# A head's root-mean-square norm, spread over one more slot of the attention loop of block 1

## The chip, the cores and the metric

The kernel runs on one core of a Trainium2 chip. The metric is the device time of one execution in microseconds. Lower is better.

## The reference, cut to what matters

The program computes two transformer blocks one after the other, all in fp32. The change touches only the first, which has two layers (0 and 1). In each layer attention has eight heads of a first kind (A) and four of a second kind (B), and only the second kind has a norm of its own:

```
def diff_attend(q1, q2, k1, k2, v, lam):        # heads of the second kind, 4 of them
    p = softmax(q1 k1 / 8) - lam * softmax(q2 k2 / 8)
    return p @ v                                 # 128 numbers per token and head

def mixer_outputs(o_a, o_b, ga, gb, p, lam_init):
    y_a = o_a.reshape(B, S, H_A * V_A) @ p['w_br_a']
    o_b = rms_norm(o_b, p['g_sub']) * (1.0 - lam_init)    # the norm of this change, over the 128
    y_b = o_b.reshape(B, S, H_B * V_B) @ p['w_br_b']
    merged = sigmoid(ga) * y_a + sigmoid(gb) * y_b
    return merged @ p['w_out']
```

Layer 0 has 512 latent and 256 context tokens as queries, layer 1 the 512 latent tokens only.

## The kernel before, in words

Every engine runs a fixed list of instructions, in order, and engines meet at semaphores. For the heads of a layer all five lists come from one list of items, `head_items` (L310 to L419), which `pe_heads`, `act_heads` and `dve_heads` walk. The list goes slot by slot. A slot is one chunk of 256 keys of one pair of query tiles (256 queries); a pair over 768 keys has three slots. In a slot stand: `scores` of tiles two or three slots ahead (q times k into PSUM; VectorE takes the row maxima at L1448, ScalarE the exponentials at L1291, and for the second kind VectorE weighs the two softmaxes together, the item `weigh`, ending at L1363); `turn` (TensorE transposes the weights, L1170; ScalarE copies the result out, L1301, and VectorE takes its low half, L1462); `values` of the slot two before (L1184 broadcasts the inverse sums, L1203 to L1205 multiply by v; after a pair's last chunk ScalarE copies the sum out, L1315, and VectorE scales it, L1479); and pieces of later work: projections of the next head (`b_qk`, 24 matmuls at L658 to L660), its rotation (`b_rope`: L1139 and L1140 on TensorE, L1431 to L1436 on VectorE, L1276 on ScalarE), early `gate` projections (24 matmuls, copied out by ScalarE at L1324), and `prepare`, the split of a weight block (L618 on ScalarE, L629 on VectorE).

The norm of a head of the second kind is four items. `ob_square`: ScalarE squares a pair's scaled sum (L1330). `ob_sum`: TensorE sums the squares over the partitions with a matrix of ones, one matmul per stream (L1217; the stream of 512 and in layer 0 also that of 256). `ob_root`: ScalarE takes the logarithm out of PSUM (L1336) and then the exponential of minus half of it (L1340), with a load of the function table ahead of each. `ob_norm`: VectorE multiplies the head by it (L1486), and the SyncE queue stores it. Heads are numbered 0 to 11; 8 to 11 are of the second kind.

Where results of `turn`, `gate`, `b_qk`, `b_rope` and `ob_sum` go is fixed by a ring, `gen = Turns([4, 5, 7])`: three PSUM banks, taken in turn in TensorE's order. Who takes a bank waits until the one before has given it back:

```
def take(self, queue, *key, place=None):
    ...
    if self.held[i] is not None and self.given_back is not None:
        name, event = self.given_back[self.held[i]]
        queue.wait_ge(self.signals[name], *event)
```

An `ob_sum` gives its bank back with the logarithm (`logged`), a `b_rope` with VectorE's addition at L1433 (`roped`), a `turn` and a `b_qk` with VectorE's reading of it (`taken`), a `gate` with ScalarE's copy (`copied`).

Of the kernel before, what the change touches and what calls it, by code (L numbers as in the profile page):

```python
# [246 lines left out]
def early_gates(streams):  # L247
    return [(m, s, g) for m in EARLY for s, g in itertools.product(streams, range(2))]
# [37 lines left out]
def pairs_of(streams):  # L286

    out = []
    for n, (kind, h) in enumerate(HEADS):
        for s in streams:  # L290
            for q0 in range(s[0], s[1], 2 * P):
                keys = N_TOK if s == LAT else N_CTX
                out.append(dict(n=n, kind=kind, h=h, s=s, q0=q0, keys=keys, chunks=keys // (2 * P), i=len(out)))
    return out
# [15 lines left out]
def head_items(layer, engine):  # L310


    streams = [LAT] if layer == DEPTH - 1 else [LAT, CTX]
    pairs = pairs_of(streams)
    slots = [(p["i"], c) for p in pairs for c in range(p["chunks"])]
    first = {i: x for x, (i, c) in enumerate(slots) if c == 0}
    per_head = len(pairs) // len(HEADS)

    def pieces(n):

        kind, h = HEADS[n]
        if kind == "A":
            steps = [[("a_q", n, h, s)] for s in streams] + [[("a_k", n, h, s)] for s in (LAT, CTX)]
            if h == 3:
                steps[len(streams) - 1].append(("prepare",))
            if h == H_A - 1:
                steps[-1].append(("prepare",))
            return steps
        steps = []
        if h == 0:  # L330
            for b in range(2):
                steps += [[("v_b", b, t)] for t in range(N_TOK // P)]
                if b == 0:
                    steps[1].append(("prepare",))
                steps[-1].append(("prepare",))
        steps += [[("b_qk", n, h, 0, s)] for s in streams] + [[("b_rope", n, h, 0)]]
        steps += [[("b_qk", n, h, 1, s)] for s in (LAT, CTX)] + [[("b_rope", n, h, 1)]]
        steps[-2].append(("prepare",))
        return steps

    plan = [dict(scores=[], pieces=[]) for _ in slots]
    start, at = [], 0
    for p in pairs:
        for a in range(2):
            t = 2 * p["i"] + a
            if p["i"] == 0:
                start.append(("scores", t))
                continue
            at = max(at, first[p["i"]] - 3 + a)
            plan[at]["scores"].append(("scores", t))  # L350
    scored = {t: x for x, slot in enumerate(plan) for _, t in slot["scores"]}
    for n in range(1, len(HEADS)):
        steps = pieces(n)
        lo = scored.get(2 * per_head * (n - 1) - 1, -1) + 1 if n > 1 else 0
        hi = scored[2 * per_head * n] - 1
        for i, step in enumerate(steps):
            plan[lo + i * (hi - lo) // len(steps)]["pieces"].append(step)

    gates = [[] for _ in slots]
    second_kind = first[H_A * per_head]  # L360
    for x, of_chunk in zip(GATE_AT[len(streams)], EARLY):
        for y, key in zip(x, [(m, s, g) for m, s, g in early_gates(streams) if m == of_chunk]):
            gates[second_kind + y].append(("gate",) + key)
        gates[second_kind + x[-1]].append(("prepare",))

    out = []
    for i, step in enumerate(pieces(0)):
        if i == len(streams):
            out += [("v_a", t) for t in range(N_TOK // P)]
        out += step  # L370
        out += [("late",) + x for x in step if x[0] in ("a_q", "a_k")]
    out += start
    second = {2 * p["i"] + a for p in pairs for a in range(2) if p["kind"] == "B"}
    late, weigh, values, ob = [], [], [], {}

    def of_values(x, i, c):

        p = pairs[i]
        out.append(("values", i, c))
        if c == p["chunks"] - 1 and p["kind"] == "B":  # L380
            ob.setdefault("ob_square", []).append((x, i))
            if (i + 1) % per_head == 0:
                for what in ("ob_sum", "ob_root", "ob_norm"):
                    ob.setdefault(what, []).append((x + 1, p["n"]))

    def of_norm(x, what):
        out.extend((what, y) for at, y in ob.get(what, ()) if at == x)

    for x, (i, c) in enumerate(slots):
        scores = plan[x]["scores"]  # L390
        if engine != "act":
            out += scores[0:1]
        out.append(("turn", i, c))
        out += late
        late = []
        of_norm(x, "ob_sum")
        values.append((i, c))
        if len(values) > 2:
            of_values(x, *values.pop(0))
        if engine == "act":  # L400
            out += scores[0:1]
        out += [("weigh", t) for t in weigh]
        weigh = [t for _, t in scores if t in second]
        of_norm(x, "ob_root")
        out += gates[x]
        late += [("gate_out",) + y[1:] for y in gates[x] if y[0] == "gate"]
        for step in plan[x]["pieces"]:
            out += step
            late += [("late",) + y for y in step if y[0] in ("a_q", "a_k")]
        out += scores[1:]  # L410
        of_norm(x, "ob_norm")
        of_norm(x, "ob_square")
    out += late
    for x, y in enumerate(values, len(slots)):
        of_values(x, *y)
        of_norm(x, "ob_square")
    for what in ("ob_sum", "ob_root", "ob_norm"):
        of_norm(len(slots) + len(values), what)
    return out  # L419


def build(nc, dram, out, book):

    with ExitStack() as ctx:
# [657 lines left out]
        def pe_heads(l):  # L1082
# [7 lines left out]
            for s in mine(l):  # L1090
                for k in range(3):
                    pe.wait_ge(taken, "cq", l, k, s)
            for item in head_items(l, "pe"):
                what, at = item[0], item[1:]
                if what == "a_q":
# [134 lines left out]
        def act_heads(l):  # L1230
            pairs = pairs_of(mine(l))
            chunks, chunk_no = chunk_numbers(pairs)
            act.wait_ge(wide_out)
            for item in head_items(l, "act"):
                what, at = item[0], item[1:]
                if what == "prepare":
# [105 lines left out]
        def dve_heads(l):  # L1342
# [22 lines left out]

            dve.wait_ge(normed, "ckv", l, 1, CTX)
            for item in head_items(l, "dve"):
                what, at = item[0], item[1:]
                if what == "prepare":
# [2064 lines left out]
```

## Time and profile before

| | us |
|---|---|
| median of 3 runs | 3739.1 (3736.39 to 3739.17) |
| span of the profiled execution | 3735.9 |
| TensorE busy | 3440.3 (92%) |
| VectorE busy | 1890.1 (51%) |
| ScalarE busy | 1431.1 (38%) |
| GpSimd busy | 309.1 (8%) |

The profiled execution has a span of 3735.9 us from its first to its last instruction, and the runs' median is 3.2 us above that. TensorE is busy nearly all the time; the others have long stretches in which they wait for it. All times in the trace are from the span's start. The second-kind heads of layer 0 lie at about 430 to 590 us, those of layer 1 at about 1720 to 1845 us.

### The profile page before, as it was taken

The page shows a single profiled execution, that of the slowest core. Times are in us where ns is not written, and L with a number is a line of the kernel's source. Part 1 is how long each engine was busy: PE and PEld are TensorE (multiplying, and loading weights), DVE is VectorE, ACT ScalarE, POOL GpSimd, SP SyncE. Part 2 cuts the span into 40 slices and gives each one's busy share as a digit, 9 for nine tenths or more (in the row PEclk, how much of TensorE's full clock was granted, in tenths as well). Part 3 has the DMA queues.
Part 4 walks back from the last instruction along what each step waited for, and adds up shares of the span by engine and source line. Part 5 has one row for each costly group of instructions (what it writes and reads, how often), then busy time and mean ns, then how long its engine had stood idle before and what let it go on. Part 6 is the DMA issues. An engine that isn't in the chain of part 4 may idle for free.

```text
span 3735.9 us, 42555 instructions
## 1 busy us (share of the span) xinstructions
PE 3440.3 (92%) x17738; PEld 2877.4 (77%) x17738; DVE 1890.1 (51%) x2678; ACT 1431.1 (38%) x2194; POOL 309.1 (8%) x242
## 2 busy tenths in 40 slices
PE   7898898999999988899799999879999888979997
PEld 6778777888888876787687888757887776758885
DVE  5674654777636545655545544544333555343233
ACT  4563444233313335534534333433222345352222
POOL 0000000221001110000011001220000200220002
PEclk9999999999999999999999999989999889999999
DMA  5101114433324321011242322212222111112222
GB/s 205 34 22 60 51 45 147 156 124 129 108 80 141 120 74 40 30 59 49 88 147 102 116 104 85 97 68 84 94 102 96 62 43 34 46 46 98 102 91 69
DMA packets 74495, 321.96 MB, mean 86 GB/s; under 512 B 8896, under 2 KB 17856, under 8 KB 52288
## 3 DMA queue, kind: packets, MB, share of 16 engines
q1 hardware_dynamic: 74304, 319.25, 24.8%
q8 instruction: 140, 2.29, 0.3%
q14 instruction: 51, 0.42, 0.0%
HBM read 303.49 MB, written 15.73 MB: 85 GB/s over the span
## 4 chain that ended last, share of the span: by engine, by line
PE 50%; DVE 4%; ACT 4%; POOL 1%; issue 1%; DMA 0%; POOLq 0%; ACTq 0%; DVEq 0%; SPq 0%
PE psum L658 14%; PE psum L660 14%; PE psum L659 14%; POOL arena L1988 1%; PE psum L1158 1%; DVE split_weights L629 1%; PE psum L671 1%; ACT split_weights L618 1%; PE psum L672 1%; PE psum L673 1%; PE psum L1170 1%; DVE arena L1448 0%; PE psum L2720 0%; PE psum L2696 0%; PE psum L1184 0%
## 5 line engine op out<-in xcount | busy, mean ns | idle before, releaser
L658 PE MATMUL psum<-split_inputs,split_weights 128*128 128x512 f32 (+1 forms) x2872 | 1054.6, 367 | 12.5 <-DVE split_weights L629 8.5
L659 PE MATMUL psum<-split_inputs,split_weights 128*128 128x512 f32 (+1 forms) x2872 | 1046.1, 364 | 0.0
L660 PE MATMUL psum<-split_inputs,split_weights 128*128 128x512 f32 (+1 forms) x2872 | 1045.0, 364 | 0.0
L629 DVE TENSOR_TENSOR split_weights<-arena,split_weights 128x2048 fp32r<-128x2048 f32 (+3 forms) x246 | 508.4, 2066 | 428.5 <-ACT split_weights L618 428.0
L658 PEld LDWEIGHTS psum<-split_inputs,split_weights 128*128 128x128 f32 x2872 | 545.2, 190 | 105.2 <-DVE split_weights L629 11.6
L659 PEld LDWEIGHTS psum<-split_inputs,split_weights 128*128 128x128 f32 x2872 | 544.9, 190 | 87.2 <-issue 3.0
L660 PEld LDWEIGHTS psum<-split_inputs,split_weights 128*128 128x128 f32 x2872 | 544.1, 189 | 86.0
L618 ACT ACTIVATE split_weights<-arena 128x2048 fp32r<-128x2048 f32 (+3 forms) x246 | 413.9, 1683 | 159.0 <-PE psum L660 158.9
L658 PE MATMUL psum<-split_hidden,split_weights 128*128 128x512 f32 (+1 forms) x880 | 324.1, 368 | 1.0 <-DVE split_weights L629 0.9
L659 PE MATMUL psum<-split_hidden,split_weights 128*128 128x512 f32 (+1 forms) x880 | 323.9, 368 | 0.0
L660 PE MATMUL psum<-split_hidden,split_weights 128*128 128x512 f32 (+1 forms) x880 | 323.7, 368 | 0.0
L2018 ACT ACTIVATE arena<-psum 128x512 f32<-128x512 f32 (+2 forms) x120 | 66.5, 557 | 367.1 <-PE psum L660 346.9
L658 PEld LDWEIGHTS psum<-split_hidden,split_weights 128*128 128x128 f32 x880 | 165.9, 189 | 29.5 <-DVE split_weights L629 2.1
L660 PEld LDWEIGHTS psum<-split_hidden,split_weights 128*128 128x128 f32 x880 | 165.9, 188 | 27.6
L659 PEld LDWEIGHTS psum<-split_hidden,split_weights 128*128 128x128 f32 x880 | 165.9, 189 | 27.5
L680 ACT ACTIVATE arena<-arena 128x512 f32<-128x512 f32 (+1 forms) x134 | 78.0, 590 | 275.9 <-DVE arena L1840 97.9
L1158 PE MATMUL psum<-split_high 128*128 128x512 f32 (+3 forms) x864 | 143.5, 366 | 43.6 <-ACT arena L1291 41.5
L1516 DVE CUSTOM_DVE_ANT_0 arena<-arena 128x1024 f32<-128x1024 f32 x128 | 165.2, 1290 | 28.2 <-DMA arena<-w_ada_dram 24.3
L1448 DVE TENSOR_REDUCE arena<-psum 128x1 f32<-128x768 f32 (+1 forms) x160 | 132.0, 846 | 77.1 <-PE psum L1158 76.2
L1158 PEld LDWEIGHTS psum<-split_high 128*128 128x128 f32 (+1 forms) x864 | 114.5, 205 | 72.9 <-ACT arena L1291 38.8
L703 POOL TENSOR_TENSOR arena<-arena 128x512 f32<-128x512 f32 x66 | 84.1, 1280 | 1002.7 <-ACT arena L680 1002.7
L1291 ACT ACTIVATE arena<-psum,arena 128x768 f32<-128x768 f32 (+1 forms) x160 | 130.2, 816 | 65.6 <-DVE arena L1448 62.4
(340 smaller groups left out, 4953.2 us busy)
## 6 DMA issues: line engine op xcount, KB each, us to landing
arena<-w_up_dram SPq DMA_DIRECT2D x44, 1024.0 KB, 5.7
arena<-ffn_up_dram SPq DMA_DIRECT2D x44, 1024.0 KB, 4.8
arena<-w_ada_dram SPq DMA_DIRECT2D x80, 512.0 KB, 3.7
arena<-w_in_dram SPq DMA_DIRECT2D x32, 1024.0 KB, 4.8
arena<-w_down_dram SPq DMA_DIRECT2D x32, 704.0 KB, 4.1
arena<-ffn_down_dram SPq DMA_DIRECT2D x32, 704.0 KB, 4.1
arena<-od_w_in_dram SPq DMA_DIRECT2D x13, 1024.0 KB, 4.9
arena<-w_ada_dram SPq DMA_DIRECT2D x8, 1024.0 KB, 12.7
```

What stands on the lines that cost most here:

```text
L618: act.e.activation(ws[:, i % N_SLOTS, 0, 0:nk * w], raw_view(key), ACT.Copy).then_inc(*w_hi(*key))
L629: dve.e.tensor_tensor(ws[:, i, 1, 0:nk * w], raw_view(key), ws[:, i, 0, 0:nk * w].bitcast(F32), ALU.subtract).then_inc(*w_lo(*key))
L658: pe.e.matmul(dst, a[0], b[0], start=i == 0, stop=False)
L659: pe.e.matmul(dst, a[0], b[1], start=False, stop=False)
L660: ins = pe.e.matmul(dst, a[1], b[0], start=False, stop=i == n - 1)
L680: act.e.activation(row, view, ACT.Square, **more).then_inc(*squared(site, s, c))
L703: pool.e.tensor_tensor(acc, acc, rows.at(site, s, c)[:, 0:w], ALU.add).then_inc(*rows.back((site, s, c), pooled, site, s, c))
L1158: ins.append(pe.e.matmul(dst, a[rows_at, :], b[rows_at, :], start=i == 0, stop=i == 2))
L1291: act.e.activation(row[:, 0:p["keys"]], psum[:, b:b + p["keys"]], ACT.Exp, bias=st[:, sub:sub + 1], accum_out=st[:, 2 + sub:3 + sub]).then ...
L1448: dve.e.tensor_reduce(st[:, sub:sub + 1], psum[:, b:b + p["keys"]], AX.X, ALU.max, negate=True).then_inc(*maxed(l, t, sub))
L1516: dve.e.tensor_tensor_reduce(part.get("junk", rstd_all), ADA[slots[n % len(slots)]], wide[:, s, :], 1.0, 0.0, ALU.mult, ALU.add, mods[al][ ...
L2018: act.e.activation(dst, banks.at(*key)[:, cols], func, **more).then_inc(*banks.back(key, copied, *key))
```

## The change

A norm whose last pair ends with `values` in slot x (where its `ob_square` also stands) was summed, rooted and scaled in slot x + 1: `ob_sum` right behind that slot's `turn`, `ob_root` in the middle, `ob_norm` near the end. Now `ob_sum` stands near the end of slot x + 1, behind its pieces of later work, and `ob_root` and `ob_norm` in slot x + 2. The last head of a layer keeps its order, so three heads in each layer (8, 9 and 10) change: six places. No instruction is added or removed.

```
         if c == p["chunks"] - 1 and p["kind"] == "B":
             ob.setdefault("ob_square", []).append((x, i))
             if (i + 1) % per_head == 0:
-                for what in ("ob_sum", "ob_root", "ob_norm"):
-                    ob.setdefault(what, []).append((x + 1, p["n"]))
+                ob.setdefault("ob_sum", []).append((x + 1, p["n"]))
+                for what in ("ob_root", "ob_norm"):
+                    ob.setdefault(what, []).append((x + 2, p["n"]))
 
     def of_norm(x, what):
         out.extend((what, y) for at, y in ob.get(what, ()) if at == x)
@@ -393,7 +394,6 @@
         out.append(("turn", i, c))
         out += late
         late = []
-        of_norm(x, "ob_sum")
         values.append((i, c))
         if len(values) > 2:
             of_values(x, *values.pop(0))
@@ -409,13 +409,16 @@
             late += [("late",) + y for y in step if y[0] in ("a_q", "a_k")]
         out += scores[1:]
         of_norm(x, "ob_norm")
+        of_norm(x, "ob_sum")
         of_norm(x, "ob_square")
     out += late
-    for x, y in enumerate(values, len(slots)):
-        of_values(x, *y)
+    for x in range(len(slots), len(slots) + len(values) + 2):
+        of_norm(x, "ob_root")
+        of_norm(x, "ob_norm")
+        if x < len(slots) + len(values):
+            of_values(x, *values[x - len(slots)])
+        of_norm(x, "ob_sum")
         of_norm(x, "ob_square")
-    for what in ("ob_sum", "ob_root", "ob_norm"):
-        of_norm(len(slots) + len(values), what)
     return out
```

Behind the diff every line number of the changed kernel is 3 higher: L1217 is L1220, L1170 is L1173, L1184 is L1187, L1139 is L1142, L1158 is L1161, L658 is L661; on ScalarE L1336 is L1339, L1340 is L1343, L1276 is L1279, L1301 is L1304, L1291 is L1294, L1324 is L1327, L1315 is L1318.

First TensorE in layer 0 around head 8's sum (L1217), from slot x + 1's transposes (L1170) to the first gate matmul of slot x + 2 (L658); the groups left out are the matmuls of `values`. Before:

```order
L1170 MATMUL psum<-arena 128x128 x3
L1217 MATMUL psum<-arena 128x512 [waits squared,taken]
L1217 MATMUL psum<-arena 128x256 [waits squared,taken]
L1184 MATMUL psum<-arena 128x128 [waits stat,scaled]
...
L1139 MATMUL psum<-split_high 128x512 [waits taken]
L1140 MATMUL psum<-split_high 128x512
L1158 MATMUL psum<-split_high 128x256 [waits exped]
L1158 MATMUL psum<-split_high 128x256 x5
L1170 MATMUL psum<-arena 128x128 [waits weighed,logged]
...
L658 MATMUL psum<-split_inputs,split_weights 128x512 [waits logged,w_lo]
```

and in the changed kernel:

```order
L1173 MATMUL psum<-arena 128x128 x3
L1187 MATMUL psum<-arena 128x128 [waits stat,scaled]
...
L1142 MATMUL psum<-split_high 128x512 [waits taken]
L1143 MATMUL psum<-split_high 128x512
L1220 MATMUL psum<-arena 128x512 [waits squared,taken]
L1220 MATMUL psum<-arena 128x256 [waits squared,taken]
L1161 MATMUL psum<-split_high 128x256 [waits exped]
L1161 MATMUL psum<-split_high 128x256 x5
L1173 MATMUL psum<-arena 128x128 [waits weighed,roped]
...
L661 MATMUL psum<-split_inputs,split_weights 128x512 [waits logged,w_lo]
```

The two sums went behind `b_rope` (L1142, L1143). The transposes of slot x + 2 now wait for `roped` where they waited for `logged`. The gate's matmul waits for `logged` in both, but the ring of three banks gives it the bank of the first sum where it had that of the second.

Then ScalarE at the same place, from the copy of slot x + 1's transposes (L1301) to the copy of the gate (L1324). Before:

```order
L1301 ACTIVATE split_low<-psum 128x512 [waits turned]
L1336 ACT_TABLE_LOAD
L1336 ACTIVATE arena<-psum,arena 128x512 [waits product]
L1336 ACTIVATE arena<-psum,arena 128x256 [waits product]
L1340 ACT_TABLE_LOAD
L1340 ACTIVATE arena<-arena 128x768 [waits logged]
L1276 ACTIVATE split_high<-arena 128x512 [waits roped]
L1301 ACTIVATE split_high<-psum 128x512 [waits turned,product]
L1291 ACTIVATE arena<-psum,arena 128x256 [waits maxed]
L1291 ACTIVATE arena<-psum,arena 128x256 [waits maxed,weighed]
L1324 ACTIVATE arena<-psum 128x512 [waits product,gate_stored_0_loaded]
```

and in the changed kernel:

```order
L1304 ACTIVATE split_low<-psum 128x512 [waits turned]
L1279 ACTIVATE split_high<-arena 128x512 [waits roped]
L1304 ACTIVATE split_high<-psum 128x512 [waits turned,product]
L1294 ACTIVATE arena<-psum,arena 128x256 [waits maxed]
L1294 ACTIVATE arena<-psum,arena 128x256 [waits maxed,weighed]
L1339 ACT_TABLE_LOAD
L1339 ACTIVATE arena<-psum,arena 128x512 [waits product]
L1339 ACTIVATE arena<-psum,arena 128x256 [waits product]
L1343 ACT_TABLE_LOAD
L1343 ACTIVATE arena<-arena 128x768 [waits logged]
L1327 ACTIVATE arena<-psum 128x512 [waits product,gate_stored_0_loaded]
```

The two logarithms and the exponential, with both table loads, went behind the copy of the next transposes and the exponentials of the next scores (L1294).

Last ScalarE at head 10 of layer 1, near the end of that layer's heads, where no gate is left. Before:

```order
L1301 ACTIVATE split_low<-psum 128x512 [waits turned]
L1336 ACT_TABLE_LOAD
L1336 ACTIVATE arena<-psum,arena 128x512 [waits product]
L1340 ACT_TABLE_LOAD
L1340 ACTIVATE arena<-arena 128x512 [waits logged]
L1301 ACTIVATE split_high<-psum 128x512 [waits turned,product] x2
L1315 ACTIVATE arena<-psum 128x256 [waits ob_stored_1_loaded,product]
```

and in the changed kernel:

```order
L1304 ACTIVATE split_low<-psum 128x512 [waits turned]
L1304 ACTIVATE split_high<-psum 128x512 [waits turned,product]
L1339 ACT_TABLE_LOAD
L1339 ACTIVATE arena<-psum,arena 128x512 [waits product]
L1343 ACT_TABLE_LOAD
L1343 ACTIVATE arena<-arena 128x512 [waits logged]
L1304 ACTIVATE split_high<-psum 128x512 [waits turned,product]
L1318 ACTIVATE arena<-psum 128x256 [waits ob_stored_1_loaded,product]
```

The group of four for the root went past one copy of transposes and stands right ahead of the next copy and of L1318, the copy of a finished pair out of PSUM.

## Rows read from the trace of the kernel before

**Rows 1.** The page: its span.

```profile
span 3735.9 us, 42555 instructions
```

**Rows 2.** Waits of TensorE, 430 to 600 us: total, times, longest.

```profile
PE psum L1158 <- ACT arena L1291: 6.2, 2, 3.1
PE psum L1217 <- ACT arena L1330: 4.7, 4, 1.4
```

**Rows 3.** Waits of TensorE, 1720 to 1846 us.

```profile
PE psum L1217 <- ACT arena L1330: 6.7, 4, 2.5
```

**Rows 4.** Timeline, TensorE, head 8 of layer 0: start, length, instructions, idle before.

```profile
456.66 0.49 PE L1139 MATMUL psum<-split_high 128*128 128x512 f32 x1 [0.70 <-DVE split_low L1462]
...
458.14 0.63 PE L1170 MATMUL psum<-arena 128*128 128x128 f32 x4 [0.19 <-DVE arena L1363]
...
459.32 0.39 PE L658 MATMUL psum<-split_inputs,split_weights 128*128 128x512 f32 x1
```

**Rows 5.** Timeline, VectorE, the same place.

```profile
456.97 1.02 DVE L1363 SCALAR_TENSOR_TENSOR arena<-arena 128x768 f32<-128x768 f32 x1
...
458.63 0.69 DVE L1433 TENSOR_TENSOR arena<-arena,psum 128x512 f32<-128x512 f32 x1
...
460.63 1.01 DVE L1486 SCALAR_TENSOR_TENSOR arena<-arena 128x768 f32<-128x768 f32 x1
461.56 0.75 DVE L1448 TENSOR_REDUCE arena<-psum 128x1 f32<-128x256 f32 x2
```

**Rows 6.** Timeline, ScalarE, the same place.

```profile
454.50 1.28 ACT L1336 ACT_TABLE_LOAD   x1
455.79 1.05 ACT L1336 ACTIVATE arena<-psum,arena 128x512 f32<-128x512 f32 x2
...
462.83 0.20 ACT L1291 ACTIVATION_READ_ACCUMULATOR arena<-psum,arena 128x1 f32 x1
```

**Rows 7.** Instructions of line L1336: shortest, median, longest in ns.

```profile
L1336 ACT ACTIVATE arena<-psum,arena x12: 468/688/692, 455.8 to 1839.8; 128x512 f32<-128x512 f32 x8, 128x256 f32<-128x256 f32 x4
```

**Rows 8.** Timeline, TensorE, head 10 of layer 0.

```profile
562.02 0.67 PE L1217 MATMUL psum<-arena 128*128 128x256 f32 x2 [1.34 <-ACT arena L1330]
...
569.26 0.62 PE L1158 MATMUL psum<-split_high 64*128 64x256 f32 x6
...
571.01 0.28 PE L658 MATMUL psum<-split_inputs,split_weights 128*128 128x256 f32 x1
```

**Rows 9.** Timeline, ScalarE, the same place.

```profile
571.80 0.21 ACT L1291 ACTIVATION_READ_ACCUMULATOR arena<-psum,arena 128x1 f32 x1
```

**Rows 10.** Timeline, TensorE, head 10 of layer 1.

```profile
1821.77 0.50 PE L1158 MATMUL psum<-split_high 64*128 64x512 f32 x2 [3.33 <-ACT arena L1291]
...
1827.04 2.05 PE L1217 MATMUL psum<-arena 128*128 128x512 f32 x2 [2.20 <-ACT arena L1330]
...
1830.76 0.60 PE L1170 MATMUL psum<-arena 128*128 128x128 f32 x4
...
1834.31 0.71 PE L1184 MATMUL psum<-arena 128*128 128x128 f32 x4 [0.62 <-DVE arena L1479]
```

**Rows 11.** Timeline, VectorE, the same place.

```profile
1828.47 1.02 DVE L1363 SCALAR_TENSOR_TENSOR arena<-arena 128x768 f32<-128x768 f32 x1
1831.79 0.75 DVE L1486 SCALAR_TENSOR_TENSOR arena<-arena 128x512 f32<-128x512 f32 x1 [2.30 <-ACT arena L1340]
...
1833.85 0.41 DVE L1479 TENSOR_TENSOR arena<-arena,psum 128x256 f32<-128x256 f32 x1
```

**Rows 12.** Timeline, ScalarE, the same place.

```profile
1831.13 0.63 ACT L1340 ACTIVATE arena<-arena 128x512 f32<-128x512 f32 x1
1831.66 0.58 ACT L1301 ACTIVATE split_high<-psum 128x512 fp32r<-128x512 f32 x1
```

**Rows 13.** Windows at half clock: us, busy of each engine, granted clock.

```profile
475.30:482.10 6.80, 5.48 (x27) 5.08 (x28) 3.21 (x8) 2.96 (x8) 0.00 (x0) 0.50 0.00 0
536.80:540.20 3.40, 3.25 (x17) 2.85 (x18) 0.95 (x2) 0.32 (x2) 0.00 (x0) 0.50 0.03 7
```

More of the change, by code:

```diff
@@ L382, in of_values @@
             if (i + 1) % per_head == 0:
-                for what in ("ob_sum", "ob_root", "ob_norm"):
-                    ob.setdefault(what, []).append((x + 1, p["n"]))
+                ob.setdefault("ob_sum", []).append((x + 1, p["n"]))
+                for what in ("ob_root", "ob_norm"):
+                    ob.setdefault(what, []).append((x + 2, p["n"]))
     def of_norm(x, what):
@@ L395, in head_items @@
         late = []
-        of_norm(x, "ob_sum")
         values.append((i, c))
@@ L411, in head_items @@
         of_norm(x, "ob_norm")
+        of_norm(x, "ob_sum")
         of_norm(x, "ob_square")
     out += late
-    for x, y in enumerate(values, len(slots)):
-        of_values(x, *y)
+    for x in range(len(slots), len(slots) + len(values) + 2):
+        of_norm(x, "ob_root")
+        of_norm(x, "ob_norm")
+        if x < len(slots) + len(values):
+            of_values(x, *values[x - len(slots)])
+        of_norm(x, "ob_sum")
         of_norm(x, "ob_square")
-    for what in ("ob_sum", "ob_root", "ob_norm"):
-        of_norm(len(slots) + len(values), what)
     return out
```

## The prediction

> **What bounds the kernel now.** I read the views in this order: the page, the waits of TensorE in the two stretches where the changed heads lie, then the timelines of TensorE, VectorE and ScalarE at each of the six places. The page gives the span, 3735.9 us [rows 1]; TensorE is busy for 3440.3 us of it, so what delays TensorE delays the end, unless a later wait of TensorE on something that is not behind it takes the delay up. In the heads of layer 0 the reader sees what the change is aimed at: TensorE waits 4.7 us in four pieces at the norm's sums for ScalarE's squares [rows 2], and in layer 1 another 6.7 us in four [rows 3]. Of the eight pieces six belong to heads 8 to 10 and two to head 11, which keeps its order. So less than 4.7 + 6.7 = 11.4 us stand at the moved instructions. The timelines then show what TensorE would wait for next if those waits were gone: at head 8 of layer 0 it stops 0.70 us for VectorE's low half of the transposes and 0.19 us for its weighing [rows 4].
>
> **The change part by part.** No instruction is added or removed. What moves is the sum (12 matmuls in the program, of which 9 move), and with it who holds which of the three banks; then the two table loads, the logarithms, the exponential, the scaling and the store. I go through the places.
>
> *Head 8 of layer 0 (and head 9, whose rows repeat these some 60 us later).* TensorE skips the first wait of 1.37 us and does the head's `values` and `b_rope` at once. The second sum then needs the bank of slot x + 1's transposes, which VectorE gives back where L1139 could start before, at 456.66 [rows 4]. So nothing is won there: scores 58 start about where they did. Now the transposes of slot x + 2. Before, they got the bank of the first sum, long given back. Now they get that of `b_rope`, which VectorE gives back when L1433 ends, 458.63 + 0.69 = 459.32 [rows 5]. A semaphore from VectorE takes some 0.15 us (L1363 ends at 456.97 + 1.02 = 457.99, and TensorE goes on at 458.14 [rows 4, 5]), so they start at 459.5 instead of 458.14, 1.3 us late. VectorE doesn't get later, since all it does up to there depends on itself and on ScalarE.
>
> Then the gate. From the transposes to the gate TensorE needs 459.32 - 458.14 = 1.18 us [rows 4], so it is at the gate at 460.7. The gate needs the bank of the first sum, which the logarithm gives back, and the logarithm now stands behind the exponentials of scores 58. Those come earlier than before, because L1486 no longer stands ahead of the maxima on VectorE: 461.56 - 460.63 = 0.93 us [rows 5]. ScalarE's last row there ended at 462.83 + 0.20 = 463.03 [rows 6], so now at 462.1. Then a table load of 1.28 us [rows 6], the first logarithm of 0.69 us [rows 7] and a semaphore: 462.1 + 1.28 + 0.69 + 0.15 = 464.2. The gate starts at 464.2 instead of 459.32: **4.9 us late**, of which 3.5 us are idle in one piece. For heads 8 and 9 of layer 0 that makes 9.8 us. The cover that hid the root before was TensorE's own work from the sums to the gate and an idle ScalarE; now the root starts 7.6 us after 454.50 and has none. The gate's 24 matmuls hide the second load, the exponential, L1486 and the store on the SyncE queue. What stands behind the store there, the store of the gate's result, waits for the gate anyway.
>
> *Head 10 of layer 0.* No `b_rope` here, and a gate follows `values` at once. Its bank is free, so TensorE doesn't wait 1.34 us at the sum [rows 8] and reaches scores 70 at 569.26 - 1.34 = 567.9. ScalarE's last exponential row ended 571.80 + 0.21 - 569.26 = 2.75 us after those scores began [rows 8, 9], so at 570.65 now; with load, logarithm and semaphores (1.28 + 0.69 + 0.15) the gate's bank is free at 572.8, where the gate started at 571.01 [rows 8]: **1.75 us late**, 3.1 us idle in one piece.
>
> *Head 8 of layer 1.* One stream and one sum. The sum goes behind `b_qk`, 24 matmuls, and its wait, the smallest (2.5 and 2.20 of the 6.7 us stand elsewhere [rows 3, 10], and head 11 has a part), is gone. But ten microseconds later VectorE is behind: the next low halves and maxima follow on a weight split, and L1486, 0.75 us long [rows 11], now stands in that row of work instead of ahead of it. I count a gain of 0.1 us.
>
> *Head 9 of layer 1.* The wait of 2.5 us at the sum [rows 3] shrinks to 1.3 us, since ScalarE splits a weight block ahead of the squares and `values` fills no more than 1.2 us; behind the scores, the transposes wait for VectorE's weighing, which is not moved. It ends when it did. 0 us.
>
> *Head 10 of layer 1.* No gate follows. The 2.20 us at the sum and the slow 2.05 us of the sum [rows 10] go; the next transposes are set free by the weighing, 1828.47 + 1.02 + 0.15 = 1829.64 [rows 11], not at 1830.76 [rows 10], 1.1 us early. But the root now stands right ahead of what the pair's end needs. ScalarE begins their copy some 0.7 us later and has them by 1830.95, then comes load, logarithm, load, exponential, 1.28 + 0.69 + 1.28 + 0.63 = 3.9 us [rows 6, 7, 12], to 1834.85. Behind it wait the next copy of transposes (0.58 us [rows 12]) and the copy L1315, and on VectorE behind L1486 (0.75 us) a low half (0.7 us, as the 0.69 us of L1433 at the same width [rows 5]) and L1479 (0.41 us [rows 11]), for which TensorE waits at L1184. 1834.85 + 0.75 + 0.7 + 0.41 gives 1836.7 with its semaphores, where L1184 started at 1834.31 [rows 10]: **2.4 us late**, all of it on the way to the end of the layer's heads.
>
> Sum without the clock: 9.8 + 1.75 - 0.1 + 0 + 2.4 = 13.8 us.
>
> *The clock.* The two stops of 3.1 us at L1158 in layer 0's heads [rows 2] are both followed by a stretch at half clock (1.2 instead of 2.4 GHz), with 5.48 and 3.25 us of TensorE's work in it [rows 13], of which half, 2.7 and 1.6 us, is lost. The stop of 3.33 us in layer 1 was followed at once by matmuls at full speed [rows 10], so a stop this long costs between 0 and 2.7 us; the mean of the three is 1.4 us. The change makes four such stops: 3.5, 3.5, 3.1 and, at head 10 of layer 1, 3.3 us. The first three have a long gate behind them and I count 1.4 us each, 4.3 us; the last has little work behind it, and I count nothing. The Trainium skill ("TensorE: Matmul & The Clock Gate", Terms) puts the penalty at the throttled time times one minus K/N, so at half of it; by that and the trace it is the same price.
>
> Total: 13.8 + 4.3 = 18.1 us over the profiled execution, whose own runs lie 3.2 us above its span (3739.1 - 3735.9). 3739.1 + 18.1 = **3757 us**.
>
> A place where page and trace differ: the load stands in the new wait three times and twice in the last place. The rows show 1.28 us, and the logarithm follows 454.50 + 1.28 + 0.01 later [rows 6]. The Trainium skill ("ScalarE: Activation LUTs", What ACT_TABLE_LOAD costs) adds a drain of about 1.38 us to each switch, 2.66 us in all. By the page the delay would be 5 x 1.38 = 6.9 us more, 3764 us; the trace has no such gap, and I go by the trace.
>
> **The rivals.** *The banks don't decide, and the waits are gone (faster).* If the logarithm of the first sum ended before TensorE reached the gate, the gain would be what VectorE's weighing leaves of the waits at the sums: 1.3 us at head 10 of layer 0 and 1.1 us at head 10 of layer 1, up to the whole 11.4 us: 3728 to 3736.7 us. For it speaks that the waits at the sum are real and that ScalarE is the least busy of the three. It decides at 460.7: the logarithm must have ended by then, and it would have to end 3.5 us earlier than its order allows, since an engine doesn't pass an instruction that waits. 4 in 100.
>
> *The delay is taken up later (within 0.2%).* The next stops of TensorE, 3.1 us at L1158 [rows 2], would have to shrink by what the gate is late. They would if ScalarE or VectorE were behind there; but both wait for TensorE's gate right before, so the whole row of work moves. Or two of the steps fail: head 8 and 9 of layer 0 at 2 us each make 3739.1 + 4 + 4 - 1.3 = 3745 us. 6 in 100.
>
> *Main case, slower*: 90 in 100. Its own bounds are 3739.1 + 13.8 = 3752.9 with no loss of clock and 3739.1 + 13.8 + 4 x 2.7 = 3763.7 with the dearest at each stop.
>
> **How the numbers follow.** The runs tell a change from none at about 0.2%, 7.5 us. The predicted time is the main case's. The range goes from 3749 us (one of the two big stalls 4 us smaller than worked out, without loss of clock) to 3764 us. Of 10 in 100 outside the main case nearly all lie below it, and some 8 in 100 of the main case outside its bounds. Faster 4, same 6, slower 90 in 100.
>
> **What the changed profile would show.** In the waits of TensorE, L661 (the gate) for ScalarE's logarithm L1339, three times, 3.5, 3.5 and 3.1 us; L1173 for VectorE's rotation (L1436 in the new numbers) two times, 1.3 us; nearly nothing at L1220 in layer 0 for the squares; L1187 in layer 1 for L1482, over 3 us once. Half-clock stretches behind some gates. What would make it wrong: a gate that starts right behind `values`, or later stops at L1161 that are shorter than before by what the gates lost.

## The result, and the profile after

The changed kernel takes 3759.04 us (median of 4 runs, 3755.66 to 3759.23); the kernel before took 3738.86 us beside it. The ratio is 1.0052, 95% interval 1.0037 to 1.0066: slower by 20.2 us. The profiled execution has a span of 3757.3 us, 21.4 more than before [rows 1].

TensorE's waits in the second-kind heads of layer 0, which lie at 430 to 610 us now; total, times, longest:

```profile
PE psum L661 <- ACT arena L1339: 9.6, 4, 2.9
PE psum L1161 <- ACT arena L1294: 6.2, 2, 3.1
PE psum L1173 <- DVE arena L1436: 2.9, 2, 1.5
PE psum L1220 <- DVE split_low L1465: 2.3, 1, 2.3
PE psum L1220 <- DVE split_high L1465: 2.3, 1, 2.3
PE psum L1220 <- ACT arena L1333: 0.6, 1, 0.6
```

The wait of the sums for the squares fell from 4.7 us [rows 2] to 0.6 us, head 11's. In its place stand the sum's wait for VectorE's low half of the transposes (4.6 us, which took in the 1.4 us of heads 8 and 9 at L1139, 0.70 us each [rows 4]), the transposes' wait for the rotation (2.9 us) and the gate's wait for the logarithm (9.6 us, of which 1.8 us is the merge's first gate, as before).

Head 8 of layer 0, TensorE's timeline (start, length, idle before and its releaser):

```profile
455.06 0.70 PE L1220 MATMUL psum<-arena 128*128 128x256 f32 x2 [2.28 <-DVE split_low L1465]
...
457.77 1.12 PE L1173 MATMUL psum<-arena 128*128 128x128 f32 x4 [1.46 <-DVE arena L1436]
...
462.63 0.77 PE L661 MATMUL psum<-split_inputs,split_weights 128*128 128x512 f32 x1 [2.47 <-ACT arena L1339]
```

and ScalarE's:

```profile
460.29 0.20 ACT L1294 ACTIVATION_READ_ACCUMULATOR arena<-psum,arena 128x1 f32 x1
460.51 1.28 ACT L1339 ACT_TABLE_LOAD   x1
461.80 1.05 ACT L1339 ACTIVATE arena<-psum,arena 128x512 f32<-128x512 f32 x2
```

This execution came to these heads 1.6 us earlier than the one before. With that, L1173 is 457.77 - 458.14 + 1.6 = 1.2 us late and the gate 462.63 - 459.32 + 1.6 = 4.9 us [rows 4]. The three rows of ScalarE are the chain to read: last exponential row, load, logarithm, with nothing between them, and the gate right behind the first of the two logarithms. Head 9 repeats it.

Head 10 of layer 1, TensorE's timeline:

```profile
1843.57 0.63 PE L1173 MATMUL psum<-arena 128*128 128x128 f32 x4 [1.56 <-DVE arena L1366]
...
1850.61 1.23 PE L1187 MATMUL psum<-arena 128*128 128x128 f32 x4 [3.00 <-DVE arena L1482]
```

From the transposes freed by the weighing to the values of the last pair there are 1850.61 - 1843.57 = 7.04 us now, where there were 1834.31 - 1830.76 = 3.55 us [rows 10].

And the clock, in windows (length, busy time of TensorE, its weight loads, VectorE, ScalarE and GpSimd, then the granted clock):

```profile
456.70:466.90 10.20, 6.66 (x20) 5.53 (x21) 3.95 (x7) 6.60 (x11) 0.00 (x0) 0.50 0.18 76
482.00:485.40 3.40, 3.38 (x29) 3.13 (x30) 2.06 (x3) 1.62 (x4) 0.00 (x0) 1.00 0.02 5
1849.30:1856.10 6.80, 5.07 (x22) 4.77 (x22) 1.95 (x4) 1.59 (x5) 0.00 (x0) 0.50 0.10 39
```

The first is a stretch at half clock (1.2 of 2.4 GHz) that the kernel before doesn't have at this place: it begins between the new stops and reaches into the gate. The second lies right behind the next stop of 3.09 us at L1161. There the clock is full now; the kernel before had half clock behind the same stop [rows 13]. The third begins in the stop of 3.00 us at L1187 and outlasts it by 5.5 us.

Where the 21.4 us of the two profiled executions lie, by the same five marks in each (the first 3.09 us stop at L1158, the first gate of layer 0's merge, the 2.11 us stop at which layer 1's second-kind heads begin, the first gate of layer 1's merge, the end):

| stretch | before, us | changed, us | more |
|---|---|---|---|
| up to 417.23 / 415.59 | 417.2 | 415.6 | -1.6 |
| heads of layer 0, up to 590.24 / 602.60 | 173.0 | 187.0 | +14.0 |
| up to 1656.29 / 1668.41 | 1066.1 | 1065.8 | -0.2 |
| heads of layer 1, up to 1840.62 / 1859.10 | 184.3 | 190.7 | +6.4 |
| the rest | 1895.3 | 1898.2 | +2.9 |

The first, the third and the last stretch hold no changed instruction, and half clock differs in them: 37.5 us in the first stretch before and 34.1 us now, 161.3 and 174.1 us in the last. So up to 3 us either way comes without any change of the lists in that stretch. A second trace of the changed kernel, on another chip, gives 187.0 and 190.8 us for the two stretches of heads, so these two are the change's. It also gives 1898.2 us for the last stretch again: whether part of its 2.9 us comes with the change is not shown.

### The profile page after: what moved, and what is told of

Its sections match the earlier page's. It is cut to its first block, busy times and chain, and to the rows that moved or that the text cites. A ratio compares the mean times of both kernels' runs of the same rounds, so it can differ in the third digit from the quotient of the medians.

```text
span 3757.3 us, 42554 instructions
## 1 busy us (share of the span) xinstructions
PE 3452.1 (92%) x17738; PEld 2887.2 (77%) x17738; DVE 1889.8 (50%) x2678; ACT 1429.6 (38%) x2194; POOL 308.5 (8%) x242
## 4 chain that ended last, share of the span: by engine, by line
PE 50%; DVE 4%; ACT 4%; POOL 1%; issue 1%; DMA 0%; POOLq 0%; ACTq 0%; DVEq 0%; SPq 0%
PE psum L661 14%; PE psum L662 14%; PE psum L663 14%; POOL arena L1991 1%; PE psum L1161 1%; DVE split_weights L632 1%; PE psum L674 1%; PE psum L675 1%; PE psum L676 1%; PE psum L1173 1%; ACT split_weights L621 1%; PE psum L2699 0%; DVE arena L1451 0%; PE psum L2723 0%; PE psum L1187 0%
## 5 line engine op out<-in xcount | busy, mean ns | idle before, releaser
L661 PE MATMUL psum<-split_inputs,split_weights 128*128 128x512 f32 (+1 forms) x2872 | 1057.3, 368 | 20.3 <-ACT arena L1339 9.6
L661 PEld LDWEIGHTS psum<-split_inputs,split_weights 128*128 128x128 f32 x2872 | 547.1, 190 | 113.8 <-issue 12.0
L661 PE MATMUL psum<-split_hidden,split_weights 128*128 128x512 f32 (+1 forms) x880 | 324.2, 368 | 0.1
L661 PEld LDWEIGHTS psum<-split_hidden,split_weights 128*128 128x128 f32 x880 | 165.9, 189 | 28.6 <-DVE split_weights L632 0.9
L1161 PE MATMUL psum<-split_high 128*128 128x512 f32 (+3 forms) x864 | 142.5, 363 | 43.6 <-ACT arena L1294 41.4
L1161 PEld LDWEIGHTS psum<-split_high 128*128 128x128 f32 (+1 forms) x864 | 113.6, 203 | 73.9 <-ACT arena L1294 38.8
L1294 ACT ACTIVATE arena<-psum,arena 128x768 f32<-128x768 f32 (+1 forms) x160 | 130.0, 815 | 62.4 <-DVE arena L1451 58.3
```

The source lines that it names most:

```text
L661: pe.e.matmul(dst, a[0], b[0], start=i == 0, stop=False)
L1161: ins.append(pe.e.matmul(dst, a[rows_at, :], b[rows_at, :], start=i == 0, stop=i == 2))
L1294: act.e.activation(row[:, 0:p["keys"]], psum[:, b:b + p["keys"]], ACT.Exp, bias=st[:, sub:sub + 1], accum_out=st[:, 2 + sub:3 + sub]).then ...
```

## The experiments

The first four ran on one chip beside the kernel before (3738.21 us). Theory A is that of the prediction: TensorE waits for banks and copies that the late root holds up. Each kernel's edit is to the changed kernel unless it says otherwise.

**Root ahead of the next transposes.**

```
+        of_norm(x, "ob_root")
         out.append(("turn", i, c))
...
-        of_norm(x, "ob_root")
         out += gates[x]
```

> The changed kernel with one edit: the root stands at the start of slot x + 2, ahead of that slot's transposes, so ScalarE takes the logarithms before it copies the transposes and before the exponentials of the next scores. The sum stays late. Theory A (the root is late, and holds the gate's bank in layer 0 and the end of head 10 in layer 1): the gates of heads 8 and 9 in layer 0 start some 2.2 us earlier each, that of head 10 2.9 us, and L1187 behind head 10 of layer 1 2.6 us, 9.9 us in all, and with fewer stretches at half clock 14 us: 3745 us, 3742 to 3749. The waits of TensorE for roped (1.46 us, two times) stay. Rival B (the late sum itself is what costs, by its place ahead of the scores): nothing changes, 3756 to 3760 us.

3745.59 us, ratio to before 1.0021 (1.0012 to 1.0031): 13 us less than the changed kernel, as theory A said. TensorE, head 8 of layer 0 (this execution is 3.4 us behind the changed kernel's from the start):

```profile
463.95 0.76 PE L661 MATMUL psum<-split_inputs,split_weights 128*128 128x512 f32 x1 [0.36 <-ACT arena L1339]
```

The stop at the gate went from 2.47 to 0.36 us and that at L1187 behind head 10 of layer 1 from 3.00 to 1.59 us. Layer 0's heads take 179.9 us in place of 187.0, layer 1's 186.0 in place of 190.7. The sum stands as late as in the changed kernel, so rival B falls: where the root stands is what costs most. Not all of it, for 7.4 us above the kernel before remain, and the transposes still wait 2.9 us for the rotation in layer 0.

**The gate in another bank.**

```
                     if s == LAT and g == 0:
                         w_gate = pe_block("w_in", l, 6 + H_B + m)
+                    if summed and l == 0:     # the first gate behind an ob_sum
+                        gen.n += 2            # the bank of the last transposes
+                    summed = False
                     pe_gate(l, m, s, g, w_gate, gen.next())
...
```

> The changed kernel with one edit: in layer 0 the first gate behind a norm's sum takes the bank that the last transposes used, not that of the sum; all lists stay in their order. Theory A1 (the gate waits for nothing but the bank that the late logarithm holds): it starts when VectorE has read the transposes, 2.1 us earlier at heads 8 and 9 and some 2 us at head 10, 6.3 us, and with fewer stretches at half clock 10 us: 3749 us, 3746 to 3753. Rival C (the order on ScalarE is itself the delay, whatever the bank): the gates start where they did, 3756 to 3760 us.

3755.74 us, ratio 1.0042 (1.0027 to 1.0057), 2.7 us above my range. But the waits are as theory A1 has them. TensorE, head 8:

```profile
460.65 0.77 PE L661 MATMUL psum<-split_inputs,split_weights 128*128 128x512 f32 x1 [0.35 <-DVE split_high L1470]
```

The gate starts 2.0 us earlier and waits for VectorE's reading of the transposes; the logarithm is no longer in it. Rival C falls. Layer 0's heads take 181.4 us, 5.6 us less than the changed kernel's. My estimate was 10 us, of which 3.7 us by the clock, and that part I had mis-sized: half clock stands behind both 3.09 us stops here, where the changed kernel has none. Of the 5.6 us another 2.2 us went again in the stretch behind layer 0's heads, 1068.0 us against 1065.8, which holds no edit.

**One layer at a time.** The change for layer 0 alone, then for layer 1 alone:

```
+                ob.setdefault("ob_sum" if layer == 0 else "ob_sum_first", []).append((x + 1, p["n"]))
                 for what in ("ob_root", "ob_norm"):
+                    ob.setdefault(what, []).append((x + 1 + (layer == 0), p["n"]))
...
+        out.extend(("ob_sum", y) for at, y in ob.get("ob_sum_first", ()) if at == x)
```

> The change in layer 0 only; layer 1 keeps the order of before. By the traces of both kernels the layer's heads take 14.0 us longer, with stretches at half clock included: 3752.5 us, 3750 to 3755. Should most of the loss be from layer 1 or from later stages, it is under 3748 us.

3751.45 us, ratio 1.0034 (1.0022 to 1.0047).

> The change in layer 1 only. My sum gives 2.3 us without the clock, the trace of the changed kernel 6.5 us with two stretches at half clock that the kernel before hadn't in these places: 3743 us, 3741 to 3746. If those stretches depend only on where the stops lie in time, the value is near 3741; if they follow from the change in layer 1, near 3745.

3745.59 us, ratio 1.0014 (1.0004 to 1.0023). Layer 0's heads take 187.0 us in the first and 173.0 in the second, layer 1's 184.3 and 190.7: each layer has its own loss to 0.1 us, and the two medians' distances from before, 13.2 and 7.4 us, add up to 20.6, the whole 20.2 within their intervals. Layer 1 is dearer than my 2.3 us, and by its own doing: both stretches at half clock are there with layer 0 unchanged. TensorE at L1187 (here L1189) behind head 10 of layer 1:

```profile
1836.97 0.58 PE L1189 MATMUL psum<-arena 128*128 128x128 f32 x1 [3.00 <-DVE arena L1484]
```

**The clock.** Two kernels on a second chip (before: 3736.61 us), the changed one again and one whose new stops in layer 0 are filled with matmuls that add zeros to the open sum of the values:

```
+            def refill(n):
+                for _ in range(2 * n):
+                    pe.e.matmul(o[0:64, 0:P], ident[0:64, 64:P], ones[0:64, :], start=False, stop=False)
...
+                if what == "turn" and fill:      # 3 at heads 8 and 9
+                    refill(fill.pop(0))
+                elif what == "gate" and fill:    # 6 at heads 8, 9 and 10
+                    refill(fill.pop(0))
...
+                        if s == CTX and n in (8, 9):
+                            refill(4)
```

> The changed kernel unchanged, as the measure for the kernel with filled stops on the same chip: 3757 to 3760 us.

3761.37 us (3757.33 to 3762.55), ratio 1.0064 (1.0052 to 1.0077), 1.4 us above the range.

> The changed kernel with added matmuls of TensorE that add zeros to the open sum of the values (the result stays as it was): 8 of them ahead of the second norm sum, 6 ahead of the next transposes and 12 ahead of the gate at heads 8 and 9 of layer 0, 12 ahead of the gate at head 10; by the duration of a like pair (0.47 us) they take 1.9, 1.4 and 2.8 us, about what TensorE idles there. Theory K (part of the loss is the half clock that follows these stops): the stretches at half clock behind the gates are gone, and the layer's heads, 187 us in the changed kernel's trace, take 181 to 184 us, the lower if those behind the 3.1 us stops don't come back; 3753 to 3757 us. Rival L (half clock comes by its own times and not from these stops): the heads take 187 us or longer, since the filling overshoots the gate by some 0.3 us each: 3759 to 3761 us.

3753.16 us (3749.68 to 3756.62), ratio 1.0048 (1.0034 to 1.0062): more work on TensorE, and 8.2 us less. The first gate and the window around it:

```profile
462.60 0.47 PE L661 MATMUL psum<-split_inputs,split_weights 128*128 128x512 f32 x1 [0.75 <-ACT arena L1355]
```

```profile
456.70:466.90 10.20, 9.44 (x63) 8.12 (x62) 3.92 (x7) 6.72 (x11) 0.00 (x0) 1.00 0.19 80
480.50:483.90 3.40, 3.40 (x20) 3.11 (x18) 2.04 (x3) 0.93 (x2) 0.00 (x0) 0.50 0.00 0
```

The gate starts at the same time as in the changed kernel (462.63), so the filling moved nothing, and the window that had half clock has full. Theory K holds for these stops. But the second row shows half clock back behind the 3.09 us stop, so layer 0's heads are only 2.4 us shorter (184.6 us, where I expected 181 to 184), and the rest of the 9.3 us between this profiled execution (span 3748.0 us) and the changed kernel's lies in stretches that hold no filling. So only 2.4 us are shown to come from the filled stops; that the median fell into my range owes more to the other stretches. The stops trade stretches with each other.

**The sum behind the values, the rest as before.** This asks what the squares' wait is worth. Both kernels are edits to the kernel before and ran on the second chip (before: 3736.61 us); in the second, sum and root go behind the gate at head 10 of layer 0:

```
-        of_norm(x, "ob_sum")
         values.append((i, c))
         if len(values) > 2:
             of_values(x, *values.pop(0))
+        of_norm(x, "ob_sum")
```

> The kernel before with one edit: the norm's sum stands behind the slot's values, not ahead of them; root and scaling stay where they were. Theory A (the squares' wait is real but in most places the next thing TensorE waits for ends at the same time): in layer 0 nothing at heads 8 and 9, where the transposes' bank and the weighing are next, 0.5 us at head 10; in layer 1 0.1 us at head 8, nothing at head 9, 1.1 us at head 10; 1.7 us together: 3735 to 3738 us where before gives 3738.2. Rival M (the waits at the sum are worth what they show): 9 us, 3729 us.

3740.7 us, ratio 1.001 (1.0001 to 1.0019).

```
+                late_sum = y < len(slots) and bool(gates[y]) and not plan[y]["pieces"]
+                ob.setdefault("ob_sum_late" if late_sum else "ob_sum", []).append((y, p["n"]))
+                ob.setdefault("ob_root_late" if late_sum else "ob_root", []).append((y, p["n"]))
+                ob.setdefault("ob_norm", []).append((y + late_sum, p["n"]))
...
```

> As the kernel with the sum behind the values, but at head 10 of layer 0, where a gate and no rotation stands in the slot, sum and root stand behind that gate and the scaling one slot later. Theory A: TensorE finds the squares ready and the next gate's bank free there, 1.0 to 1.3 us less than with the kernel before at that place instead of 0.5 us: 3734 to 3737 us. If the root at the slot's end holds up the next transposes' copy, the gain turns into a wait at the next values: 3738 us or above.

3742.55 us, ratio 1.0015 (1.0006 to 1.0024). Both missed: slightly slower, where I expected slightly faster. Rival M is far off, though: of the 4.7 us of waits at layer 0's sums 3.7 us are gone, and nothing came of it. First the wait for the second sum of head 8 in the kernel before, then the same place and head 10 in the first of the two:

```profile
454.13 0.67 PE L1217 MATMUL psum<-arena 128*128 128x256 f32 x2 [1.37 <-ACT arena L1330]
```

```profile
456.05 0.50 PE L1139 MATMUL psum<-split_high 128*128 128x512 f32 x1 [1.86 <-DVE split_low L1462]
...
561.76 0.38 PE L1184 MATMUL psum<-arena 128*128 128x128 f32 x1 [0.66 <-DVE arena L1479]
```

The 1.37 us of before and the 0.70 us at L1139 [rows 4] became one stop of 1.86 us that ends at the same instruction, and at head 10 a wait for VectorE's scaling comes forward that I had not seen. The stretches at half clock differ from before's: a new one of 3.4 us behind the first 1.86 us stop, 6.8 where 3.4 us stood at two later stops, and 3.4 where 6.8 us stood at one. In all, the heads of the two layers have 51.4 us of half clock where before had 44.4, and take 174.5 and 185.4 us where before took 173.0 and 184.3. Whether the clock is what was lost, the next three kernels ask.

**All the stops filled** (before on this chip: 3737.57 us). Filling goes into the bank that the ring gives next:

```
+SPARE = {(0, 48): 20, (0, 49): 12, (0, 55): 12, (0, 61): 12, (0, 67): 12,
+         (1, 33): 8, (1, 35): 18, (1, 39): 18, (1, 43): 18, (1, 47): 13}
...
+            def spare(n):          # after the wait for that bank's last holder
+                for _ in range(n):
+                    pe.e.matmul(banks.views[b][:, 0:P], ident, ones, start=True, stop=True)
...
                 elif what == "scores":
                     t, = at
+                    spare(SPARE.get((l, t), 0))
```

> The kernel before with added matmuls of TensorE (ones through the identity, into the bank that the ring gives next; nobody reads them) ahead of those second-kind scores at which its trace shows TensorE idle 2 to 7 us for ScalarE's exponentials: 20 and 12 at tiles 48 and 49 of layer 0, 12 at tiles 55, 61 and 67; 8, 18, 18, 18 and 13 at tiles 33, 35, 39, 43 and 47 of layer 1; 0.235 us each at full speed, always less than the stop. Theory K (half clock follows a stop, and costs): the stretches at half clock behind these stops go, 30.7 us of them in layer 1's heads and some 27 in layer 0's, half of that less what lay in the stops: 10 to 18 us, 3720 to 3729 us. Rival L (filling does nothing for the clock): 3737 to 3741 us, since the filling fits in the stops.

3726.78 us (3725.24 to 3729.14), ratio 0.9971 (0.996 to 0.9983): 10.8 us faster than before with nothing but useless matmuls added. In the traces the stretches with filling are 3.7 us (up to the first heads of the second kind in layer 0), 5.6 us and 7.4 us (the heads of the two layers) shorter, and the two stretches without are 3.0 and 3.2 us longer.

The windows around two of the stops that were 3.09 and 4.50 us long:

```profile
467.00:480.00 13.00, 12.79 (x88) 10.99 (x87) 6.33 (x11) 5.30 (x11) 0.00 (x0) 1.00 0.06 21
...
1713.00:1725.00 12.00, 11.32 (x75) 9.71 (x74) 8.57 (x14) 5.99 (x13) 0.00 (x0) 1.00 0.47 168
```

> The kernel with the sum behind the values, with the same filling and 7 zero-adding matmuls ahead of the rotation at heads 8 and 9 of layer 0. If what it lost on the kernel before (4 us) was half clock behind its stops of 1.86 us and 3.3 us, it is now 0 to 2 us faster than the filled kernel before: 3719 to 3728 us. If the sum's place itself costs, it stays 4 us above it.

3722.82 us (3720.8 to 3725.72), ratio 0.9962 (0.9948 to 0.9976). With the stops filled in both, moving the sum behind the values is 4.0 us faster, not 4 us slower. So the sum's place was not what cost. How much of the 4.0 us the new place earns is less clear. In the traces layer 0's heads (from the weighing's wait at L1170 near 375 us to the merge) are 0.4 us shorter, with no half clock in either from the first second-kind scores on. Layer 1's are 2.5 us shorter, but the filled kernel before still has 6.8 us of half clock in them and this one 0.2 us; in the last stretch it is 170.6 and 164.5 us. Some of the gain is therefore clock again. This is the best version found, 14.8 us below the kernel before on that chip, and some 0.9% below the changed one by their ratios to it.

> The changed kernel with all of that filling, that of its own new stops included and 12 ahead of the values behind head 10 of layer 1. With the clock up in both, what is left between it and the filled kernel before is the delay of the lists alone, 13.8 us by my sum and 14 to 15 us by the trace: 3735 to 3743 us. Were the delay mostly clock, under 8 us would be left.

3742.7 us (3738.5 to 3744.91), ratio 1.0012 (1.0003 to 1.002). (Ahead of the gates of heads 8 and 9 it has 10 added matmuls, not 12.) That is 15.9 us above the filled kernel before. In the traces layer 0's heads take 219.0 against 206.6 us (from near 375 us to the merge), layer 1's 159.8 against 157.0 (from the stop of 4.7 us to the merge): 12.5 and 2.8 us. The two profiled executions as a whole are 11.5 us apart, as the stretch between the heads and the last one are 2.5 and 3.0 us shorter here. From their first second-kind scores on the heads of layer 0 have no half clock in either, and of layer 1 it is the filled kernel before that has more, 6.8 us against 3.4. The delay is in the lists; the clock is not most of it. The gate of head 8, in the filled kernel before and in this one:

```profile
454.37 0.39 PE L659 MATMUL psum<-split_inputs,split_weights 128*128 128x512 f32 x1
```

```profile
461.18 0.47 PE L662 MATMUL psum<-split_inputs,split_weights 128*128 128x512 f32 x1 [1.18 <-ACT arena L1369]
```

The scores that open layer 0's second-kind heads start at 413.87 and 415.72 us, so the gate comes 40.5 us behind them in the one and 45.5 us in the other: 5.0 us late with the clock full in both.

## Why the prediction was right, point by point

The direction, the mechanism and the size held: 3757 us forecast, 3759.04 measured.

- *Nothing is won at the first sums.* Right: the second sum waits where L1139 had waited, and the transposes came 1.2 us late (1.3 forecast), freed by the rotation.
- *The gate waits for the first logarithm, 4.9 us late, three times in layer 0.* Right to 0.1 us: at head 8 in the changed kernel itself, at both heads in the filled pair (5.0 and 4.9 us). The stop is 2.47 us and not 3.5, because TensorE, already at half clock, was later at the gate; its start is what I had worked out. At head 10 the gate is 2.4 us late in the filled pair, not 1.75: I had missed that `values` there waits 0.66 us for VectorE's scaling (L1482), so not the whole 1.34 us at the sum is won. The bank kernel shows that the bank is the wait; the root kernel shows that it is held by the root's place.
- *Head 8 and 9 of layer 1, -0.1 and 0 us.* Right: TensorE is 0.9 us ahead behind head 8's sum and has given back 0.7 of it at L1187 (1.91 us there, 1.25 before) some 20 us later; head 9 changes nothing.
- *Head 10 of layer 1, 2.4 us late.* Right without the clock. My chain from the transposes to the values gave 1836.7 - 1829.64 = 7.06 us and the changed kernel has 7.04; in the filled pair the values come 14.9 us behind the scores at the 3.3 us stop (L1158 before), against 12.5, so 2.4 us late. In the changed kernel itself the 1.1 us that I had let the weighing win are not there: half clock ahead of the transposes made them 0.9 us late (9.84 us behind those scores, before 8.99), and the values 4.3 us.
- *Sum without the clock, 13.8 us.* 12.5 + 2.8 = 15.3 us by the filled kernels' traces. The first number is free of half clock; the second is not, since in layer 1 the filled kernel before has 3.4 us more of it.
- *The clock, 4.3 us.* The term that was mis-sized. In layer 0 it is 14.0 - 12.5 = 1.5 us: each gate did lose some 2 us, but the stops of 3.09 us behind them kept full clock, where before they had lost as much. In layer 1, where I counted nothing, it is 6.4 - 2.8 = 3.6 us: a longer stretch at the unchanged 3.3 us stop and a new one behind the 3.0 us stop. I had taken that 3.3 us stop of before for one that costs nothing; but a stretch at half clock of 3.4 us began 5 us behind it, and the sum's 2.05 us [rows 10] are its mark. Together 5.1 us, near my 4.3 by two errors that cancel; so the close total is partly luck, while the terms of the lists are not.
- *The faster rival* would have needed the logarithm 3.5 us earlier. *The rival of no change* would have needed shorter stops at L1161: they are 6.2 us in both kernels. (Its two half-sized steps add up to 3745.8 us, not 3745.)

What stays open: which stop is followed by half clock in a given execution. I can say what the filling does, not what decides it.

## What to carry to other kernels

Before moving a step later to spare a wait, write down who holds what it needs to give back: a bank from a ring is released by the step's last reader, and if that reader goes behind two exponentials on its own engine, the ring's next taker waits for them too. A wait that vanishes is worth only what the next wait behind it leaves; here 3.7 us of waits at three heads' sums were worth 0.4 us in layer 0, because transposes and weighing ended at the same time. Where an engine's stops cost clock, compare orders with the stops filled, otherwise a step that costs nothing can look like a loss of 4 us.

## What the runs showed of the hardware

TensorE's own useless work made the program faster: 143 added matmuls of 128 x 128 took 10.8 us off. Half clock (1.2 of 2.4 GHz) summed up to 286 us in the profiled execution before and 251 us in the filled one. The Trainium skill ("TensorE: Matmul & The Clock Gate", HAM oscillation) tells of a kernel that loses clock to waits between bursts of matmuls; the traces agree in the main, with stops of 2 to 5 us here, though not every such stop is followed by half clock. Less expected was how such stretches trade places: filling the stops at the gates brought half clock back behind a stop of 3.09 us that had been free of it.

The load of ScalarE's function table took 1.28 us with the logarithm right behind it (460.51 + 1.28, then 461.80), in its new place too, where the wait for the gate makes it count in full. Nothing stands between the load and its neighbours at head 8 in either kernel; the longer price that the prediction weighed, which led to 3764 us, was not paid.
